# A two-layer attention and mixture-of-experts trunk: who splits the output weights, who copies keys, how empty blocks are passed, and what is issued first

## What is computed

```python
for l in range(DEPTH):                       # DEPTH = 2, x is 1024 tokens x 1024
    h = rms_norm(x, norm1_gain[l]); z = h @ w_in[l]
    q, k, v, u = split(z)                    # 512 columns each
    att  = dilated_attention(rope(rms(q)) * scale, rope(rms(k)), v)   # 8 heads x 64, causal
    pool = pool_mixer(u, w_pool[l], pool_scale[l])   # trailing means over 2/4/8/16 tokens
    x = x + concat(att, pool) @ w_out[l]
    x = x + hier_moe(rms_norm(x, norm2_gain[l]), ...)
    # 1 of 4 groups, then 2 of its 4 experts: each token visits 2 of 16 experts
```

## Time and profile before

| what | value |
|---|---|
| three timed runs | 1656.7, 1650.93, 1657.66 us (median 1656.7) |
| the profiled execution | 1649.49 us, span 1647.7 us |
| mean granted TensorE clock in it | 0.941 of 2.4 GHz |
| TensorE busy | 1423.5 us (86%) |
| VectorE busy | 981.6 us (60%) |
| ScalarE busy | 668.8 us (41%) |
| GpSimd busy | 352.6 us (21%) |
| chain that ended last | PE 62%, DMA 15%, issue 9%, DVE 8%, ACT 3% |

### The profile page before, as it was taken

The page is one execution under the profiler, slowest core; times in us unless marked ns, Lnnn a source line. Parts: engine busy times, 40 slices in busy tenths (PEclk is TensorE's granted clock), DMA queues, the critical chain, the costliest instruction groups (busy, mean ns, idle before and its releaser), DMA issues.

```text
span 1647.7 us, 23889 instructions
## 1 busy us (share of the span) xinstructions
PE 1423.5 (86%) x7323; PEld 1138.3 (69%) x7324; DVE 981.6 (60%) x1859; ACT 668.8 (41%) x1028; POOL 352.6 (21%) x204
## 2 busy tenths in 40 slices
PE   6999997998994799999299999879989938999981
PEld 5888876887883566666188787768868826666650
DVE  6666677564446656665376756676534485666560
ACT  4332164662211455555332323646611124555540
POOL 1000059002000133332610000940100011332325
PEclk9999998999997799999699999989999969999995
DMA  8100020000139599974770002000001665899927
GB/s 308 40 1 1 1 103 1 2 1 14 51 119 340 175 319 294 336 203 102 165 240 1 1 1 92 12 1 1 1 13 78 231 226 164 262 285 329 278 45 129
DMA packets 115885, 204.63 MB, mean 124 GB/s; under 512 B 9816, under 2 KB 76576, under 8 KB 115776
## 3 DMA queue, kind: packets, MB, share of 16 engines
q1 hardware_dynamic: 90976, 130.77, 23.1%
q0 software_dynamic: 19136, 53.67, 14.7%
q10 hardware_dynamic: 5664, 18.88, 2.9%
HBM read 169.72 MB, written 49.28 MB: 133 GB/s over the span
## 4 chain that ended last, share of the span: by engine, by line
PE 62%; DMA 15%; issue 9%; DVE 8%; ACT 3%; DVEq 2%; POOL 1%; ACTq 0%; POOLq 0%; SPq 0%
PE ps L1523 19%; DMA out_x<-x_res,arena 13%; PE ps L1658 10%; PE ps L1502 9%; PE ps L1611 7%; PE ps L1739 6%; PE ps L1754 4%; PE ps L1585 2%; PE ps L1587 2%; PE ps L1675 2%; DVE arena L1284 1%; DVEq L1394 1%; DVE xgT_lo L1398 1%; PE ps L1645 1%; DVE w_in_lo L1054 1%
## 5 line engine op out<-in xcount | busy, mean ns | idle before, releaser
L1389 DVE TENSOR_TENSOR gu_lo<-big,gu_hi 128x2048 fp32r<-128x2048 f32 x96 | 217.9, 2291 | 167.4 <-ACT gu_hi L901 153.7
L1523 PE MATMUL ps<-w_in_hi,hT_hi 128*128 128x512 f32 x512 | 204.9, 400 | 14.1 <-DVE w_in_lo L1054 9.4
L674 POOL DMA_INDIRECT x_res<-token_rows,row_tok x62 | 101.3, 1634 | 504.3 <-issue 305.6
L1523 PE MATMUL ps<-w_in_hi,hT_lo 128*128 128x512 f32 x512 | 201.5, 393 | 0.0
L1523 PE MATMUL ps<-w_in_lo,hT_hi 128*128 128x512 f32 x512 | 200.9, 392 | 0.0
L901 ACT ACTIVATE gu_hi<-big 128x2048 fp32r (+1 forms) x96 | 181.2, 1916 | 37.1 <-PE ps L1739 37.1
L1502 PE MATMUL ps<-cst,arena 128*128 128x128 f32 x970 | 149.6, 281 | 44.2 <-DVE arena L1184 19.2
L1502 PEld LDWEIGHTS ps<-cst,arena 128*128 128x128 f32 x970 | 117.1, 144 | 92.2 <-issue 21.9
L1739 PE MATMUL ps<-gu_hi,xgT_hi 128*128 128x512 f32 x360 | 150.3, 418 | 23.7 <-DVE xgT_lo L1398 23.6
L1754 PE MATMUL ps<-big,arena 128*128 x360 | 165.5, 603 | 4.8 <-issue 4.8
L1174 DVE CUSTOM_DVE_ANT_0 arena<-ps,cst 128x128 f32<-128x128 f32 (+7 forms) x128 | 96.6, 755 | 96.3 <-PE ps L1587 95.6
(11 more groups left out here) (179 smaller groups left out, 2367.8 us busy)
## 6 DMA issues: line engine op xcount, KB each, us to landing
big<-in_w_gate SPq DMA_DIRECT2D x32, 1024.0 KB, 9.5
big<-in_w_up SPq DMA_DIRECT2D x32, 1024.0 KB, 14.5
big<-in_w_down SPq DMA_DIRECT2D x32, 1024.0 KB, 14.2
big<-in_w_in SPq DMA_DIRECT2D x14, 1024.0 KB, 9.9
big<-in_w_out SPq DMA_DIRECT2D x4, 2048.0 KB, 10.2
token_rows<-arena ACTq DMA_DIRECT2D x16, 512.0 KB, 2.7
out_x<-x_res ACTq DMA_DIRECT2D x16, 512.0 KB, 3.6
x_res<-out_x SPq DMA_DIRECT2D x8, 512.0 KB, 5.4
```

The costliest lines, as they stand in the source:

```text
L674: pool.indirect_dma_start(out=xg[slot], out_offset=None, in_=token_rows, in_offset=bass.IndirectOffsetOnAxis(ap=row_tok[:, j:j + 1], axis= ...
L1389: ve.tensor_tensor(out=gu_lo[i], in0=raw, in1=gu_hi[i].bitcast(f32), op=ALU.subtract)\
L1523: ins = te.matmul(ps[:, 2 + 2 * par_ + i, :], a[par_][:, k, :], b[:, k, :], start=k == 0 and n == 0, stop=k == K - 1 and n == 2)
```

## The change

It does five things. (1) Of `w_out`, the first 5120 of 8192 columns are no longer split by GpSimd but in five slices of 1024 columns, at row 3 of heads 3 to 7 on ScalarE (high part, from m = 27) and at row 4 on VectorE (low part, from m = 28); the last 3072 stay on GpSimd behind the last score. (2) The key copy of the next head goes from VectorE's row 3 to ScalarE's row 2 (`k_other`), with a semaphore of its own, `k_copied`, for which TensorE waits at the head's first row; the very first copy stays on VectorE. (3) The tests for empty blocks stand around groups of three from block 16 on: one `If(used > t)` for the group, inner tests for its second and third block, and in its `Else` one raise of each semaphore by the sum. (4) ScalarE's first loads of `w_in` stand ahead of its semaphore raises, and SyncE's raises behind its first loads. (5) VectorE makes the first half of the first low weights ahead of the first `norm_x`.

```diff
-        def steps(eng, n, body, chain=None, ring=2, sure=0, maybe=None, begun=False):
+        def steps(eng, n, body, chain=None, ring=2):
...
+        def block_steps(eng, used, body, maybe, skip):
+            body(0, 0, 0)
+            loops = (BLOCKS - 2) // RING
+            with eng.Fori(0, SURE) as j:
+                for i in range(1, RING + 1):
+                    body(RING * j + i, i % RING, j + i // RING)
+            def group(t, m, n):
+                with eng.If(used > t):
+                    body(t, 1, m)
+                    for i in range(1, n):
+                        maybe(t + i, (1 + i) % RING, m + (1 + i) // RING)
+                with eng.Else():
+                    skip(t, m, n)
+            with eng.Fori(SURE, loops) as j:
+                group(RING * j + 1, j, RING)
+            group(1 + RING * loops, loops, BLOCKS - 1 - RING * loops)
@@ sync
-            sp.sem_inc(gu_loaded, BIAS)
-            sp.sem_inc(dn_loaded, BIAS)
-            sp.sem_inc(spare_may, BIAS)
             sp.dma_start(xr[:, 0, :], x[0, 0:P, :]).then_inc(s_x[0], 16)
             sp.dma_start(ident, consts[:, C_ID:C_ID + P]).then_inc(s_id, 16)
...
+            sp.sem_inc(gu_loaded, BIAS)
+            sp.sem_inc(dn_loaded, BIAS)
+            sp.sem_inc(spare_may, BIAS)
             load_in(0, 1, 2)
@@ gpsimd
-                split_out(0, 0, K * 512).then_inc(wo_split, 1)
-                split_out(1, 0, K * 512 - H1)
                 pool.wait_ge(s_done, upto(l, 16 * PAIRS, 16 * PAIRS))
                 pool.sem_inc(s_passed, 1)
-                split_out(1, K * 512 - H1, K * 512).then_inc(wo_split, 1)
+                split_out(1, K * 512 - H1, K * 512).then_inc(wo_rest, 1)
@@ scalar
-            for s in (params, q_high_in, ...
+            for g in range(2):
+                k = slice(g * K // 2, (g + 1) * K // 2)
+                a_.dma_start(raw_in[0][:, k, :], w_in[0, :, 0:512].rearrange("(k p) n -> p k n", p=P)[:, k, :])\
+                    .then_inc(s_win[0][g], 16)
+            for s in (params, wo_top, k_copied, q_high_in, ...
...
+                def k_other(p, a):
+                    own, other = heads(a)
+                    sc.activation(k_high[a][other, :], kT[own, p, :], ACT.Copy).then_inc(k_copied, 1)
...
+                    if n == 2:
+                        k_other(p, 1)
+                    w = (m - 27) // T
+                    if m >= 27 and i == 3:
+                        if w == 0:
+                            a_.wait_ge(pooled, upto(l, NG, NG))
+                        a_.wait_ge(s_wout[w // 4], (l + 1) * 16)
+                        c = slice(w % 4 * SEQ, (w % 4 + 1) * SEQ)
+                        sc.activation(w_o_hi[w // 4][:, c], w_o[w // 4].rearrange("p k n -> p (k n)")[:, c], ACT.Copy)\
+                            .then_inc(wo_top, 1)
                     if p < PAIRS - 1:
+                        if n == 10:
+                            k_other(p + 1, 0)
...
-                steps(a_, BLOCKS, moe_act, ring=RING, sure=SURE, maybe=maybe_act)
+                def skip_act(t, m, n):
+                    maybe_down(t - 1, 0, m)
+                    a_.sem_inc(silu_done, n)
+                    a_.sem_inc(aT_ready, n)
+                    a_.sem_inc(gu_top, halves_ahead(t, n))
+                    a_.sem_inc(xg_top, rows_ahead(t, n))
+                    a_.sem_inc(y1_ready, n - 1)
+                block_steps(a_, used, moe_act, maybe_act, skip_act)
@@ vector
             gain1(0, 0, 0)
+            in_low(0, 0, [0])
             norm_x(0, 0, 0)
-            in_low(0, 0)
+            in_low(0, 0, [1])
...
+                    w = (m - 28) // T
+                    if m >= 28 and n % T == 4:
+                        dve.wait_ge(wo_top, upto(l, 5, w + 1))
+                        c = slice(w % 4 * SEQ, (w % 4 + 1) * SEQ)
+                        ve.tensor_tensor(out=w_o_lo[w // 4][:, c], in0=w_o[w // 4].rearrange("p k n -> p (k n)")[:, c],
+                                         in1=w_o_hi[w // 4][:, c].bitcast(f32), op=ALU.subtract).then_inc(wo_split, 1)
...
                         if n % T == 2:
-                            k_lower(q, a, 2 * q + a + 2)
-                        if n % T == 3:
-                            k_copy(q, a).then_inc(staged, 1)
+                            k_lower(q, a, 2 * q + a + 2).then_inc(staged, 1)
@@ tensor
                         pe.wait_ge(staged, upto(l, 2 * PAIRS, m // T + 1))
+                        if m:
+                            pe.wait_ge(k_copied, upto(l, 2 * PAIRS - 1, m // T))
...
                     if first(t):
-                        pe.wait_ge(wo_split, upto(l, 2, 2))
+                        pe.wait_ge(wo_split, upto(l, 5, 5))
+                        pe.wait_ge(wo_rest, upto(l, 1, 1))
...
+                def skip_pe(t, m, n):
+                    pe.wait_ge(xtm_done, upto(l, BLOCKS, t + 1))
+                    pe.sem_inc(xtm_done, rows_ahead(t, n))
+                    maybe_down(t - 1)
+                    pe.sem_inc(gu_half, n)
+                    pe.sem_inc(gu_done, n)
+                    pe.sem_inc(a_t_done, n)
+                    pe.sem_inc(dn_done, n - 1)
```

More of the change, by code:

```diff
@@ L395, in steps, with halves_ahead, rows_ahead @@
                 body(t, t % ring, t // ring)
+        def block_steps(eng, used, body, maybe, skip):
+            body(0, 0, 0)
+            loops = (BLOCKS - 2) // RING
[12 more added lines that the diff above has]
+            group(1 + RING * loops, loops, BLOCKS - 1 - RING * loops)
+        def halves_ahead(t, n):
+            return sum(0 if last(t + i, BLOCKS) else 1 if near_end(t + i, BLOCKS) else 2 for i in range(n))
+        def rows_ahead(t, n):
+            return sum(not last(t + i, BLOCKS) for i in range(n))
         SURE = (2 * SEQ // P - 1) // RING
@@ L587, in _ @@
             pool.wait_ge(s_ms, 2)
-            for s in (x_ready, pooled, wo_split):
+            for s in (x_ready, pooled, wo_rest):
                 pool.sem_inc(s, BIAS)
```

51 lines of the change are left out of this document (24 added, 27 removed).

## The result

The changed kernel takes 1629.81 us, median of four runs (1625.79 to 1636.38), against 1657.18 us of the kernel before (1650.93 to 1657.77, four runs). The ratio is 0.9847 with a 95% interval of 0.9803 to 0.9891. A second comparison of the two, made beside the last experiments (6 and 17 runs), gives 0.987 (0.9843 to 0.9897). By these ratios 25.4 and 21.5 us of 1657 are gone.

The account below looks back on a forecast made before the run. TensorE was taken to lead the chain, losing time to idling and low clock in attention and between layers. Terms -29.4 + 1.6 - 3.4 - 1.3 = -32.5 us, set against 1653.8, gave 1621 us; range 1606 to 1637.

Parts of the forecast that it names:

- Attention, what goes: Slow heads lose VectorE's waits for GpSimd: third heads 9.2 and 11.2 us, second 3.8, first 0.7 per layer; 29.4 us gained.
- Attention, what comes: Work moved to ScalarE and VectorE is mostly covered; the key copy sticks out 0.11 us per head, costing 1.6 us.
- Between the layers: Passing empty blocks in groups lets TensorE start layer 2 sooner, but ScalarE is late next: 3.4 us won, not 9.8.
- TensorE saves six raises and keeps the 2.88 us branch: Between the layers, TensorE saves 9.8 us on empty blocks and reaches the transposes at about 807 instead of 816.38 us.
- The step on `gain1`: Between the layers, `gain1` begins at 828.8 instead of 830.51 us and ends at 832.3; TensorE had reached tile 1 at 835.8.
- Start: Loads ahead of raises and an earlier first low half let TensorE begin sooner: 1.3 us gained, bounds 0 and 2.9.
- End: After 1636 us only DMA works; scatters of empty places set the end, so 0 change, bounds -0.5 and +2.9.
- The collisions move: Rival, 1636 us, chance 0.12: in attention `q_low` and `k_lower` still wait for GpSimd's pooling; four waits cost 14.8 us.
- ScalarE takes the path: Rival, 1666 us, chance 0.03: two copies in one head make ScalarE late for TensorE, ten heads at 4.4 us each.
- More is won: Rival, 1607 us, chance 0.08: full 9.8 us between layers, all excess of second and third heads, no cost; 46.6 us.
- it does nothing: Rival, 1652 us, chance 0.03: the copy was never the cause, or TensorE's wait for `k_copied` replaces the old one.

Follow-up runs that it names:

- both halves: Two kernels made from the kernel before: only the weight split moved off GpSimd (1626.47 us, 0.9874); only the key copies moved to ScalarE (1629.54 us, 0.9856).
- the two edits that took the gap back: Changed kernel with key copies two rows later (0.9901); changed kernel with row 2's copy back on VectorE and tile 1's square earlier (0.9776; without groups 0.9781).
- The run with the square ahead: Changed kernel with ScalarE's square and root of x tile 1 ahead of its copy of the last half of the first weights: 1620.86 us, 0.982.

## Why the prediction was right or wrong

The predicted 1621 us missed the measured 1629.81 by 9 and its range of 1606 to 1637 held it. The sum behind it, -32.5 us, was too large: 25.4 and 21.5 us were measured, 13.1 between the two profiles. Two of its terms, between the layers and at the start, had the wrong sign. Against the two profiles the sum is 19 us off, against the two ratios 7 to 11: that the total came out nearer than its terms is luck. Profile to profile, by its terms:

- *Attention, what goes.* Forecast -29.4, measured -27.0: first three heads -0.37 - 3.64 - 8.45 in layer 1 and -0.38 - 3.69 - 10.50 in layer 2. The second head's 3.8 was right (3.64, 3.69), the 9.2 and 11.2 nearly, the first head's 0.7 was 0.37. The mechanism, a VectorE copy that waits for a GpSimd operation to end, was shown by both halves. What I had not seen is that either half alone would do for the third head, and that the `k_lower` of the third head was held too (3.67 us, beside GpSimd's one-input copy).
- *Attention, what comes.* Forecast 1.6, measured 6.9 in the profiles (0.3 in layer 1; 4.9 in layer 2, and 1.7 more in pooling and projection behind a seventh head at the low clock). This is a mis-sized term, and the main one. I counted the 0.11 us by which the copy sticks out (in 14 heads, which makes 1.5 and not 1.6, though only six of them have `att_t`), and it did so by 0.16; I left out that the `att_t` gap is where the clock falls, though my own rows 2 held the case of 21.65 us. By the means of all profiles the longer gap costs 1.6 us in the fifth and seventh heads (22.1 against 20.5), 6.4 us in four of them, and the third heads have the same gap. That the longer gap makes the slow heads more frequent rests on these counts, those of the two edits that took the gap back among them; why it does so these runs don't show.
- *Between the layers.* Forecast -3.4, measured +3.75 (67.20 to 70.95), +4.5 in the second execution. The step "TensorE saves six raises and keeps the 2.88 us branch" was half right: transposes come 7.0 us sooner, not 9.4. The way from the last block to the long branch fell by 8.9 us (12.1 to 3.3), but that branch, over three bodies, took 5.29 us, 2.4 more, while the one to the head of the layer loop took 5.49, 1.0 less. The step on `gain1` failed. I had named ScalarE's load as the next in the line and then let `gain1` begin at 828.8, with the load and ScalarE's branch as long behind the last block as in the kernel before. That is 35.7 us behind it, and it measured 40.3. Counted from the end of the last block, the load was issued 1.6 us later than before (800.35 - 789.12 = 11.2 against 802.73 - 793.06 = 9.7), behind an add that took 7.62 us to land instead of 6.04, and ScalarE could begin 17.8 us behind its issue instead of 16.1; then it idled 3.76 us at its layer branch instead of 2.57. What TensorE gained it spent waiting for that; why the add and the load took longer I haven't settled. The run with the square ahead, which took that wait out of the line, had tile 1 3.9 us sooner, and VectorE's branch stood right behind.
- *Start.* Forecast -1.3, measured +2.8 in this profile and +1 in the mean. The step that failed is that the weights are what is waited for. The first low half began at 13.53 us instead of 13.06 although its load was issued sooner, because the gains that `gain1` needs came 1.7 us later (7.67 for 5.94).
- *End.* Forecast 0, measured -0.9; over all profiles 34.1 to 37.0, so nothing.
- *The blocks*, which I gave no term: +5.1 in layer 1 and -3.8 in layer 2. The changed kernel's second execution has +0.3 and -3.7.

The sum of the measured is -27.0 + 6.9 + 3.75 + 2.8 + 1.3 - 0.9 = -13.2, of 13.1.

The rivals. *The collisions move* was real and small: `k_lower` waited in the first head (3.28 us, at 230.83) and in the third (2.46) at no price, `q_low` in the second (1.92, at 248.60), and the run without pooling prices all of it at 0.7 us per layer. *ScalarE takes the path* had its mechanism right and its condition wrong. One copy stands there, not two, and already brings part of it; two copies cost all that the change had won. My argument against it, that ScalarE idles 5.4 us in a head, did not bear on it: where `att_t` stands only the 0.94 us in that one row counted. *More is won* and *it does nothing* fell.

The Trainium skill, page SBUF — State Buffer, section Who interferes with whom, says that a VectorE operation with two SBUF inputs contends with a GpSimd one that reads SBUF. Beside two-input GpSimd operations the rows agree: `q_low` that began 0.10 us behind one of 2.39 us took 3.38 us instead of 1.22. So they do beside GpSimd's one-input copy (`k_lower` 3.67 us instead of 1.21). Beside its one-input scaling they do not: `q_low`, begun at 228.73 inside one of 2.8 us, took its 1.22.

## What to carry to other kernels

Find the slack of an engine in the one row where its work is wanted, not in its idle time over a stage. A gap of TensorE behind which the clock already falls now and then can cost whole microseconds more when it is stretched by a tenth (here from 1.67 to 1.83 us). When two edits attack the same wait from both sides, make each alone first: here either gave the gain, and one of ScalarE's two key copies could then be left out. An engine that is let through earlier gains only as far as the next load that is issued behind the same event; follow that chain to its end, branches of the other engines included, before a number is written down.

## What the runs showed that I had not expected

- A gap of 1.83 us in place of 1.67 ahead of eight transposes: low clock in 19 of 28 heads against 6 of 24, for 1.6 or 3.1 us each.
- TensorE's long branch between the layers took 5.29 us over three block bodies (3.43 to 6.30 in nine profiles with the groups) and 2.88 over a single one.
- Small loads came later when the bulk weights of another queue were issued ahead of them: with the weights first the gains reached TensorE at 7.67 to 8.05 us in nine profiles, and with the old order at 5.14 to 5.94 us in five.
- A VectorE operation with two inputs was hardly held by GpSimd's one-input scaling of 2.76 us: `k_lower` began inside one and took 1.50 us, 0.29 over its time alone. GpSimd's one-input copy of 4.69 us did hold it, for 2.46 us.
